# Turning the output sums of two attention mixers with transpositions, and adding their parts on GpSimd

## The reference, cut to what matters

```python
def block(q_blk):                                   # mixer A, 128 queries at a time, 8 heads, 2 key/value heads
    sc = jnp.einsum('bqkgd,bskd->bkgqs', q_blk, k) * scale
    pr = jax.nn.softmax(sc, axis=-1)
    return jnp.einsum('bkgqs,bskd->bqkgd', pr.astype(v.dtype), v)

e = jnp.exp(sc - mx[..., None])                     # mixer B, 8 heads, three dilated windows (1024 key slots per tile)
den = jnp.sum(e, axis=-1)
o = jnp.einsum('brnqhk,brnkhd->brnqhd', e.astype(vs.dtype), vs) / den[..., None]
```

## Time and profile before

| | |
|---|---|
| median of 3 runs | 3668.93 us (3666.88 to 3674.45) |
| profiled execution | 3670.11 us, its span 3667.2 us |
| TensorE matmul busy | 3467.2 us, 95% of the span |
| VectorE, ScalarE, GpSimd busy | 2394.2, 1890.3, 1877.0 us |
| mixer A, steady loop | about 508 to 1281 us of the span |
| mixer B, steady loop | about 1305 to 1760 us |
| feed phase (output projection, MLP, gate) | from about 1791 us |

### The profile page before, as it was taken

The page is one execution under the profiler, slowest core; times in us unless marked ns, Lnnn a source line. Parts: engine busy times, 40 slices in busy tenths (PEclk is TensorE's granted clock), DMA queues, the critical chain, the costliest instruction groups (busy, mean ns, idle before and its releaser), DMA issues.

```text
span 3667.2 us, 56161 instructions
## 1 busy us (share of the span) xinstructions
PE 3467.2 (95%) x18428; PEld 2943.7 (80%) x18428; DVE 2394.2 (65%) x4351; ACT 1890.3 (52%) x3554; POOL 1877.0 (51%) x1188
## 2 busy tenths in 40 slices
PE   7999979999999999999779998999989999899997
PEld 6878768888888889999668887788877888778885
DVE  5434558888888877788465656556565565655554
ACT  2222258888888777778353443334443344433342
POOL 4545512332000034334437777577775777757773
PEclk9999989999999999999889999999999999999998
DMA  4444334443002143344214444345453444434441
GB/s 165 163 170 157 125 105 147 154 154 131 17 17 50 24 91 79 66 90 113 85 63 155 157 145 159 112 151 161 143 162 111 153 160 143 162 109 147 147 151 55
DMA packets 288912, 444.97 MB, mean 121 GB/s; under 512 B 175188, under 2 KB 194076, under 8 KB 282684
## 3 DMA queue, kind: packets, MB, share of 16 engines
q1 hardware_dynamic: 279356, 428.51, 37.4%
q10 hardware_dynamic: 9344, 13.73, 1.0%
HBM read 377.92 MB, written 76.71 MB: 124 GB/s over the span
## 4 chain that ended last, share of the span: by engine, by line
PE 41%; DVE 6%; ACT 2%; issue 1%; POOL 0%; DMA 0%; SPq 0%; DVEq 0%; ACTq 0%
PE feed_bank L1619 41%; DVE feed_res L1927 2%; DVE feed_total L1924 1%; DVE feed_xn L1900 1%; ACT feed_xT L1777 1%; PE feed_bank L1610 1%; DVE feed_xT L1909 0%; POOL feed_w_split L1570 0%; DMA feed_y_in<-scr_yB 0%; DVE feed_ms L1888 0%; DVE feed_total L1984 0%; DVE feed_rec L1891 0%; DVE feed_comb L2011 0%; ACT feed_junk L1752 0%; DVE feed_sums L2030 0%
## 5 line engine op out<-in xcount | busy, mean ns | idle before, releaser
L1570 POOL TENSOR_TENSOR feed_w_split<-feed_w_raw,feed_w_split 128x1024 fp32r<-128x1024 f32 x424 | 1076.9, 2549 | 255.2 <-ACT feed_w_split L1805 235.9
L1619 PE MATMUL feed_bank<-feed_w_split,feed_comb 128*128 128x512 f32 x3648 | 855.1, 395 | 27.9 <-DVE feed_sums L2030 10.4
L1619 PEld LDWEIGHTS feed_bank<-feed_w_split,feed_comb 128*128 128x128 f32 x3648 | 690.8, 190 | 181.2 <-DVE feed_sums L2030 12.9
L1619 PE MATMUL feed_bank<-feed_xT,feed_w_split 128*128 128x512 f32 x3072 | 700.7, 390 | 2.5 <-DVE feed_xT L1909 2.5
L1619 PEld LDWEIGHTS feed_bank<-feed_xT,feed_w_split 128*128 128x128 f32 x3072 | 577.5, 188 | 123.2 <-DVE feed_xT L1909 2.9
L358 PE MATMUL proj_bank<-proj_w_split,proj_xT 128*128 128x512 f32 (+1 forms) x1920 | 407.2, 372 | 19.3 <-ACT proj_st L426 16.1
L358 PEld LDWEIGHTS proj_bank<-proj_w_split,proj_xT 128*128 128x128 f32 x1920 | 335.5, 190 | 86.2 <-ACT proj_st L426 20.6
L1567 POOL TENSOR_SCALAR feed_w_split<-feed_w_raw 128x1024 fp32r<-128x1024 f32 x200 | 228.1, 1140 | 340.3 <-issue 307.7
L930 DVE TENSOR_TENSOR mixa_pT<-mixa_turned,mixa_pT 128x512 fp32r<-128x512 f32 x512 | 348.0, 685 | 81.3 <-ACT mixa_pT L876 77.8
L876 ACT ACTIVATE mixa_pT<-mixa_turned 128x512 fp32r<-128x512 f32 x512 | 306.4, 599 | 150.1 <-PE mixa_turned L819 131.8
L777 PE MATMUL mixa_out_acc<-mixa_pT,mixa_v_hl 128*128 128x512 f32 x1028 | 366.2, 438 | 0.5 <-DVE mixa_pT L930 0.5
(11 more groups left out here) (191 smaller groups left out, 5155.8 us busy)
## 6 DMA issues: line engine op xcount, KB each, us to landing
feed_w_raw<-w_tail_dram SPq DMA_DIRECT2D x200, 512.0 KB, 3.6
feed_w_raw<-scr_wT SPq DMA_DIRECT2D x160, 512.0 KB, 3.3
proj_w_raw<-w_in_dram SPq DMA_DIRECT2D x39, 1024.0 KB, 4.9
feed_w_raw<-w_ff_dram SPq DMA_DIRECT2D x64, 512.0 KB, 3.5
scr_table<-scr_bias SPq DMA_DIRECT2D x8, 1520.0 KB, 9.0
proj_x_t<-x_dram SPq DMA_DIRECT2D x20, 512.0 KB, 6.3
mixa_q_in<-scr_qA SPq DMA_DIRECT2D x36, 256.0 KB, 3.3
mixb_q_in<-scr_qB SPq DMA_DIRECT2D x18, 512.0 KB, 5.6
```

The lines of the kernel that those rows point to most:

```text
L1570: pool.tensor_tensor(w_sp[1][:, slot, :], w_raw[:, slot, :], w_sp[0][:, slot, :].bitcast(F32), ALU.subtract).then_inc(w_lo, 1)
L1619: mm = pe.matmul(dst, lhs, rhs, start=start, stop=stop)
```

## The change

- **TensorE.** `fold_out` issues transpositions with the 128x128 identity in place of products with `fold`: 4 per half in mixer A, 2 per unit in mixer B. The `fold` matrix and its load go. High and low parts arrive side by side in 128 columns per head.
- **VectorE.** `output` scales all 128 columns: 128x512 per half in mixer A (before 128x256), 128x256 per unit in mixer B (before 128x64), there into a new tile `y_part` with two slots of two units. Before the first unit of a slot it waits until GpSimd has emptied the slot. In mixer A the low part of the turned queries leaves VectorE.
- **ScalarE** copies the turned queries of mixer A to `q_raw` instead of to their high part.
- **GpSimd.** In mixer A `summed` becomes two additions (halves, then high and low), and `query_split` makes the high and low part of the turned queries. In mixer B a new `summed(h, e)`, one per two units, adds in two steps into `y_st`, which now holds two blocks of four units.
- **SyncE.** In mixer B y is stored in four DMAs per head, `store(h, c)` with c from 0 to 3. `one` begins with `store(h-1, 3)`, and `store(h, 0)` to `store(h, 2)` stand behind it.

The core of the diff (removed declarations, semaphore renames and the `fold` constant left out):

```diff
 # mixer A, GpSimd
-            def summed(count, slot, stored):
+            def summed(count, slot, stored, step_at):
                 pool.wait_ge(half_done, count * 2)
+                pool.tensor_tensor(y_half[:, 0, :], y_half[:, 0, :], y_half[:, 1, :], ALU.add).then_inc(merge, 1)
+                parts = y_half[:, 0, :].rearrange("p (h a d) -> p h a d", h=G, a=2)
+                pool.wait_ge(merge, step_at)
                 pool.wait_ge(y_out[slot], stored)
-                pool.tensor_tensor(y_st[:, slot, :], y_half[:, 0, :], y_half[:, 1, :], ALU.add).then_inc(y_done, 1)
+                pool.tensor_tensor(y_st[:, slot, :].rearrange("p (h d) -> p h d", h=G), parts[:, :, 0, :],
+                                   parts[:, :, 1, :], ALU.add).then_inc(y_done, 1)
+            def query_split(V, g):
+                pool.wait_ge(qt_raw, V + 1)
+                pool.sem_inc(step, 1)
+                pool.tensor_scalar(qT[g][:].rearrange("p h n -> p (h n)"), q_raw[:], 1.0, 0.0, ALU.mult, ALU.add
+                                   ).then_inc(qt_lo, 1)
+                pool.wait_ge(qt_lo, V * 2 - 1)
+                lower = qT[g][HD:P, :, :].rearrange("p h n -> p (h n)")
+                pool.tensor_tensor(lower, q_raw[HD:P, :], lower.bitcast(F32), ALU.subtract).then_inc(qt_lo, 1)
+                pool.wait_ge(qt_lo, V * 2)
...
-                summed(U + 1, 1 - w, it * 16 + 16)
+                summed(U + 1, 1 - w, it * 16 + 16, U * MERGE + 5)
+                query_split(U + 2, w)
 # mixer A, TensorE
-                    mm = pe.matmul(out_acc[half][:, h * HD:(h + 1) * HD], oT[:, half, h * P:(h + 1) * P], fold[:],
-                                   start=True, stop=True)
+                    mm = pe.transpose(out_acc[half][:, h * P:(h + 1) * P], oT[:, half, h * P:(h + 1) * P], ident[:])
 # mixer A, VectorE
-                                 out_acc[half][:, 0:G * HD].rearrange("p (h d) -> p h d", h=G),
-                                 factor[:, slot, half, :].unsqueeze(2).broadcast_to([P, G, HD]), ALU.mult
+                                 out_acc[half][:].rearrange("p (h d) -> p h d", h=G),
+                                 factor[:, slot, half, :].unsqueeze(2).broadcast_to([P, G, 2 * HD]), ALU.mult
...
-                        if s == 7:
-                            query_lo(U + 2, w, out_acc[1])
 # mixer B, SyncE
-            def store(h, par, n0=0, n1=NU):
-                sp.wait_ge(y_done, h * NU + n1 + 2)
+            def store(h, c):
+                sp.wait_ge(y_ready, h * 16 + (4 * c + 7))
...
             def one(h, par, nxt):
+                store(h - 1, 3)
                 load_next(h, nxt)
                 next_tables(h, par, nxt)
-                store(h - 1, 1 - par)
             load_next(0, 1)
             next_tables(0, 0, 1)
+            for c in range(3):
+                store(0, c)
             with sp.Fori(0, NHB // 2 - 1) as it:
                 for u in range(2):
-                    one(it * 2 + 1 + u, 1 - u, it * 2 + 2 + u)
+                    h = it * 2 + 1 + u
+                    one(h, 1 - u, it * 2 + 2 + u)
+                    for c in range(3):
+                        store(h, c)
 # mixer B, GpSimd
+            def summed(h, e):
+                pool.wait_ge(y_done, h * NU + (2 * e + 4))
+                pool.sem_inc(step, 1)
+                both = y_part[:, e % 2, :, :]
+                pool.tensor_tensor(both[:, :, 0:P], both[:, :, 0:P], both[:, :, P:2 * P], ALU.add).then_inc(y_ready, 1)
+                pool.wait_ge(y_ready, h * 16 + (2 * e + 4))
+                if e % 2 == 0:
+                    pool.wait_ge(y_out[e // 2 % 2], h * 32 + (e // 4 * 16 + 16))
+                pool.sem_inc(step, 1)
+                pool.tensor_tensor(y_st[:, e // 2 % 2, e % 2 * 2:e % 2 * 2 + 2, :], both[:, :, 0:HD], both[:, :, HD:P],
+                                   ALU.add).then_inc(y_ready, 1)
...
+                    summed(h - 1, 7)
                     for m in range(PRE):
                         split_pre(h + 1, 1 - par, m)
+                        if m % 2 == 1:
+                            summed(h, m // 2)
                     split_values(h + 1, 1 - par)
+                    summed(h, 4)
...
                     tables(1 - par)
+                    summed(h, 5)
+                    summed(h, 6)
 # mixer B, TensorE
-                    mm = pe.matmul(out_acc[n % 2][:, 0:HD], oT[:, n % 2, part * P:(part + 1) * P], fold[:],
-                                   start=part == 0, stop=part == 1)
+                    mm = pe.transpose(out_acc[n % 2][:, part * P:(part + 1) * P], oT[:, n % 2, part * P:(part + 1) * P],
+                                      ident[:])
 # mixer B, VectorE
-                ve.tensor_scalar(y_st[:, par, n, :], out_acc[n % 2][:, 0:HD], rden[:, n % SLOTS:n % SLOTS + 1], None, ALU.mult
-                                 ).then_inc(y_done, 1)
+                ve.tensor_scalar(y_part[:, n // 2 % 2, n % 2, :], out_acc[n % 2][:, 0:2 * P],
+                                 rden[:, n % SLOTS:n % SLOTS + 1], None, ALU.mult).then_inc(y_done, 1)
...
-                        if n == 1:
-                            ve.wait_ge(y_out[par], (h - par) * 8 + 16)
-                        output(N + 1, par if n else 1 - par, (n - 1) % NU)
+                        if n % 2 == 1:
+                            ve.wait_ge(y_ready, h * 16 + (n // 2 * 2 + 1))
+                        output(N + 1, (n - 1) % NU)
```

More of the change, by code:

```diff
@@ L152, in row_broadcast, with project_phase @@
     return bass.AP(row.tensor, row.offset, [[0, P], [1, n]])
-def project_phase(nc, x, w_in, g_pre, g_q, g_k, rope, ident_d, fold_d, rel_bias, onehot, scr, step, ident, fold):
+def project_phase(nc, x, w_in, g_pre, g_q, g_k, rope, ident_d, rel_bias, onehot, scr, step, ident):
     NCH = 9
@@ L547, in _, with mixer_a_phase @@
                                 rotated(b, 1, t)
-def mixer_a_phase(nc, scr, ident, fold, heads, w_ff2):
+def mixer_a_phase(nc, scr, step, ident, heads, w_ff2):
     NT = S // P
@@ L572, in mixer_a_phase @@
         oT = k.sb("oT", [P, 2, BANK])
-        y_half = k.sb("y_half", [P, 2, G * HD])
+        y_half = k.sb("y_half", [P, 2, G * 2 * HD])
+        q_raw = k.sb("q_raw", [P, G * P])
         y_st = k.sb("y_st", [P, 2, G * HD])
@@ L841, in query_hi, with query_out @@
                 act.wait_ge(qt_done, V + 1)
-                act.activation(qT[g][:].rearrange("p h n -> p (h n)"), bank[:], ACT.Copy).then_inc(qt_hi, 1)
+                act.activation(qT[g][:].rearrange("p h n -> p (h n)"), bank[:], ACT.Copy).then_inc(qt_raw, 1)
+            def query_out(V, bank):
+                act.wait_ge(qt_done, V + 1)
+                act.wait_ge(qt_lo, V * 2 - 2)
+                act.activation(q_raw[:], bank[:], ACT.Copy).then_inc(qt_raw, 1)
             def exponential(V, par, c):
@@ L947, in _, with mixer_b_phase @@
             output(4 * NT + 1, 1, 1)
-def mixer_b_phase(nc, scr, step, ident, fold, heads, feed, consts, chunks):
+def mixer_b_phase(nc, scr, step, ident, heads, feed, consts, chunks):
     NU = 16
@@ L978, in mixer_b_phase @@
         oT = k.sb("oT", [P, 2, 2 * P])
-        y_st = k.sb("y_st", [P, 2, NU, HD])
+        y_part = k.sb("y_part", [P, 2, 2, 2 * P])
+        y_st = k.sb("y_st", [P, 2, 4, HD])
         score = [ctx.enter_context(nc.psum_tensor(f"mixb_score{i}", [P, 2 * BANK], F32)) for i in range(2)]
@@ L1038, in _ @@
             feed.load_w(sp, chunks)
-            store(NHB - 1, 1, 0, TT)
-            for s in y_out:
-                sp.wait_ge(s, 16 * (NHB // 2 + 1))
+            store(NHB - 1, 0)
+            sp.wait_ge(y_out[0], 32 * NHB)
+            sp.wait_ge(y_out[1], 32 * NHB - 16)
             for t in range(TT):
                 feed.load_y(sp, scr, t)
-            store(NHB - 1, 1, TT, NU)
-            sp.wait_ge(y_out[1], 16 * (NHB // 2 + 2))
+            for c in range(1, 4):
+                store(NHB - 1, c)
+            for s in y_out:
+                sp.wait_ge(s, 32 * NHB + 16)
             sp.wait_ge(feed.const_in, feed.CONSTS)
@@ L1067, in _ @@
             pool.memset(rden[:, SLOTS - 1:SLOTS], 0.0).then_inc(set_done, 1)
+            pool.memset(y_part[:, 1, :, :], 0.0).then_inc(set_done, 1)
             pool.sem_inc(o_done, 1)
             pool.sem_inc(y_done, 1)
+            pool.sem_inc(y_ready, 1)
             def tables(par):
@@ L1328, in sums, with output @@
                 ve.reciprocal(rden[:, n % SLOTS:n % SLOTS + 1], den[:, n % SLOTS:n % SLOTS + 1]).then_inc(rd_done, 1)
-            def output(count, par, n):
+            def output(count, n):
                 ve.wait_ge(fold_done, count)
-                ve.tensor_scalar(y_st[:, par, n, :], out_acc[n % 2][:, 0:HD], rden[:, n % SLOTS:n % SLOTS + 1], None, ALU.mult
-                                 ).then_inc(y_done, 1)
+                ve.tensor_scalar(y_part[:, n // 2 % 2, n % 2, :], out_acc[n % 2][:, 0:2 * P],
+                                 rden[:, n % SLOTS:n % SLOTS + 1], None, ALU.mult).then_inc(y_done, 1)
```

(16 more changed lines are left out.)

42 lines of the change are left out of this document (21 added, 21 removed).

## The result

The changed kernel takes 3739.93 us (median of 4 runs, 3738.88 to 3742.48), the kernel before 3671.69 us (median of 4 runs beside it). The ratio is 1.0188, 95% interval 1.0170 to 1.0205: 1.9% slower. The prediction was 3738 us.

The account below looks back on a forecast made before the run. TensorE was taken to bound the kernel, busy 95% of the span, with VectorE close in mixer B. Terms -30.6 + 1.1 - 6 + 86 + 18.6 = +69.1 us gave 3738 us, range 3722 to 3755 (3704 to 3768 with rivals).

Parts of the forecast that it names:

- The late load: Mixer B, heads 1 to 7: loads issued behind the store stall TensorE 12.3 us each, 86 us, bounds 74 to 101.
- The clock: TensorE behind each stall: 5.3 us at clock 0.50, half of it lost, 18.6 us over seven stalls, bounds 0 and 36.
- Mixer A: TensorE alone sets the end; 65 folds of four transpositions, each 0.47 us shorter: 30.6 us less, 1.1 lost at the end.
- the mixer's end: End of mixer A: wider last output and GpSimd's extra addition stand in the open before the last store, +1.1 us.
- Mixer B's steady work: Mixer B's units apart from the stalls: 10 us less without a prepare, 4 more with one, together -6 us.
- Units with a prepare: Mixer B: prepare waits for the output, so the shorter fold buys nothing there; +0.06 us a unit, +4 us.
- Units without: Mixer B, units without a prepare: VectorE and TensorE meet, -0.15 us a unit, 10 us less, bounds nothing and 12.
- the load in time: Mixer B: inputs arrive before TensorE needs them, no stall or clock loss; 3633 us, chance 0.07.
- rival 2: Mixer B: the stall comes but TensorE's clock stays; 3719 us, chance 0.14.
- rival 3: Mixer B: the clock stays low longer behind each stall, 36 us instead of 18.6; 3755 us, chance 0.11.
- rival 4: Mixer A gives nothing because VectorE or ScalarE fall behind at the folds; +30.6 us, 3768 us, chance 0.06.

Follow-up runs that it names:

- e1: The changed kernel with only SyncE's list in mixer B reordered, next head's loads ahead of the last two stores of y: 3644.76 us, ratio 0.9919 to the kernel before.
- e2: The kernel before with only SyncE's list changed, the store of a head's y in front of the next head's loads: 3763.03 us, ratio 1.0239.
- e3: The kernel before with the changed mixer A and the old mixer B: 3646.66 us, ratio 0.9925.
- e4: The kernel before with the old mixer A, the changed mixer B and the early loads of e1: 3677.87 us, ratio 1.0006.
- e5: e1 with TensorE's prepare in mixer B behind its unit's scores and ScalarE copying output sums first: 3620.14 us, ratio 0.9854 to the kernel before.
- e6: e3, old mixer B with its fold products, with the same move of prepare and ScalarE's copy as e5: 3640.69 us, ratio 0.9909 to the kernel before.

## Why the prediction was right, step by step

- **The late load**: right in place and mechanism, shown by e1 (undone, it gives 95 us back) and e2 (alone, it costs 90 us). Predicted 7 x 12.3 = 86 us, measured 77.4; two of the seven waits, 10.0 and 10.1 us, are shorter than the low bound of 10.5. In front of the loads the second addition took 0.46 for 0.45 us, the two handovers 0.36 for 0.14, and from the store to the first load 1.06 us passed, where I had 0.54. The loads were sooner: 11.8 us from the first issue to TensorE's start, where I had summed 13.3 with the store ahead of them and the pick-up. What the store of 128 KB in front cost can't be told apart in the 11.8. The prediction also called the time from issue to boundary spare time; the loads issued at 1391.75 took 12.75 us of it, and the prepare that needs them starts at 1424.13, so some 20 us were spare.
- **The clock**: predicted 18.6 us, 13.9 by stages and 16 by the clock's records. The term mis-sized is the stretch behind a stall: 3.1 to 6.3 us, 4.3 on average, where I took 5.3 for each. The clock falls during the wait, where it costs nothing, and only the rest of the slow stretch has work in it.
- **Mixer A**: predicted -29.5 with its end, measured -26.4. The term mis-sized is the new fold: 0.44, not 0.36 us. I had read four transpositions that stand in front of values; the folds stand between scores and transpositions. 65 x (0.83 - 0.44) = 25 us. The cost of the mixer's end, +1.1, was not measured by itself.
- **Mixer B's steady work**: predicted -6, measured +0.9 (e1 against before, by stages), +3.1 (e1 against e3, by stages) and about +4 in e4's medians, none clear of noise. The saving that was forecast did not come, though TensorE's list shrank by 0.23 us a unit, more than the 0.19 of the prediction. The output is 0.48 us, not 0.415: the nearest row in width was another kind of instruction. Units with a prepare went from 3.72 to 3.87, +0.15, where I had +0.06. Units without went from 3.19 to 3.11, -0.08, where I had -0.15.
- **The sum**: the terms measured 77.4 + 13.9 - 26.4 + 0.9 = 65.8 against 69.1 predicted, since the errors of the single terms (-8.6, -4.7, +3.1, +6.9) partly cancel. The medians differ by 68.2. The rest of the profile's 72 is the 5.7 us ahead of mixer A, which e2 shows in large part without the change, and 0.5 us behind mixer B. That 3738 came within 2 us of the median is thus partly luck. The prediction's range of 3722 to 3755 is also some 3 us wider on each side than its bounds of 74 and 101 us give (3726 to 3753).
- **The rivals**: the load in time is what e1 makes of it, and the time is then 3645, 12 us above the 3633 written there; the mis-sized terms of mixer A and of mixer B's steady work are 10 of them. In the changed kernel it did not happen. The clock did not stay (against rival 2), nor did it stay low much longer (rival 3). Mixer A gave nearly all (against rival 4). The rule of the Trainium skill, "TensorE: Matmul & The Clock Gate", part 4, that transpositions don't count as work for the clock, does not show here: mixer A ran at 1.00 after the change too, with transpositions as 2432 of 4485 records (before, 2175 of 4740; the prediction's 2048 are those of the probabilities alone), and behind the wait shown above the clock came back to 1.00 after 16 records of which 8 were transpositions. A stretch of transpositions alone was not run.

What stays open: from the first prepare in a head to the first in the next, the heads of mixer B without the loop's own gap take 55.3 us before and 56.1 in e3, which has the same mixer B, and also 56.1 in e1 and e4. (Head 1, which has the loop's gap, takes 59.2 before and 58.9 in e3.) Nothing run here explains these 0.7 us. Over seven heads they come to some 5 us, as much as mixer B's steady term itself; they don't bear on the other terms.

## What to carry to other kernels

When a store is moved ahead of a load in one queue's list, look at what the store waits for: loads that went out 32 us ahead of their use became the costliest wait of the kernel without one added instruction (e2). Before shortening a step of the busiest engine, ask in which units that engine is waiting for something that the step isn't part of; there the gain is near zero until that chain is moved, as e5 against e6 shows (20 us) beside e1 against e3 (2 us, within noise). The version that came out of it, transpositions in both mixers, loads ahead of the last stores, prepare behind the scores, takes 3620.1 us, 1.5% under the kernel before.

## What the runs showed of the hardware

Start to start, a product of float32 with 64 moving columns is two records and takes 0.21 us in mixer A (0.83 / 4) and 0.18 in mixer B (0.37 / 2); a transposition with 128 columns is one record and takes 0.09 to 0.11 us in mixer A and 0.07 in mixer B (0.14 / 2). The form with twice the columns takes about half the time or less. VectorE's product with a per-row scalar from PSUM takes 0.276 us for 64 columns and 0.480 for 256; the product of two tensors takes 0.415 for 256 and 0.682 for 512. By these two widths each, both grow by about 1.05 ns a column, with a fixed part that is 0.06 us larger for the first. Four loads of 512 KB each in rows of 256 bytes took 11.8 us from the first issue to TensorE's start, 178 GB/s, with a store of 128 KB in front of them and the first loads of v behind them. The granted clock of TensorE fell from 1.00 to 0.50 some 4.6 us into a wait of 11.4 us and came back 3.6 us after its end.
